# Two transformer blocks in one kernel: x is turned in two parts, eight tiles ahead of the next matrix product and eight inside its first chunk

## The reference

```python
# first block
h = rms_norm(x, g_pre_mix) * (1.0 + scale_m) + shift_m
z = h @ w_in                       # then latent attention and gated linear attention
o = concat([o_mla, o_gla]) @ w_out
x = x + gate_m * rms_norm(o, g_post_mix)
h = rms_norm(x, g_pre_ffn) * (1.0 + scale_f) + shift_f
f = (silu(h @ w_ffn_gate) * (h @ w_ffn_up)) @ w_ffn_down      # width 5632
x = x + gate_f * rms_norm(f, g_post_ffn)
# second block: 16 meta rows are put ahead of x, 272 rows in all
m = hybrid_mixer(rms_norm(h, g_pre_mix_2)) @ w_out_2
h = h + rms_norm(m, g_post_mix_2)
g = causal_dwconv(rms_norm(h, g_pre_ffn_2) @ w_gate_2, w_ffn_conv_2)   # 3 taps
f = (silu(g) * (rms_norm(h, g_pre_ffn_2) @ w_up_2)) @ w_down_2         # width 5632
h = h + rms_norm(f, g_post_ffn_2)
```

## Time and profile before

| | us |
|---|---|
| median of three runs | 2478.99 |
| the profiled execution: its own time | 2478.26 |
| its span, first to last instruction | 2476.5 |
| TensorE busy in the span | 2337.7 (94%) |
| VectorE busy | 1523.0 (61%) |
| ScalarE busy | 1073.7 (43%) |
| mean granted TensorE clock | 0.969 of full |

### The profile page before, as it was taken

How to read it: one execution, slowest core, us unless ns; L and a number is a source line. 1 busy time by engine, 2 the same in 40 slices (tenths; PEclk the granted TensorE clock), 3 DMA queues, 4 the chain that set the end, 5 groups by cost and what they waited for, 6 DMA issues and landing times.

```text
span 2476.5 us, 41603 instructions
## 1 busy us (share of the span) xinstructions
PE 2337.7 (94%) x16266; PEld 2169.9 (88%) x16266; DVE 1523.0 (61%) x1703; ACT 1073.7 (43%) x1235; POOL 123.0 (5%) x246
## 2 busy tenths in 40 slices
PE   3999989799999999999899999997999999999997
PEld 3899668799998899988699995796999988999976
DVE  7988688645554476644645994445655644566545
ACT  5463253544443344433544436345444433344433
POOL 0000013000001100001200000000000011000010
PEclk9999999999999999999999997798999999999999
DMA  9988749555555588745464550153555555555552
GB/s 397 421 325 334 314 179 369 168 186 186 186 186 193 181 290 284 272 166 193 124 204 153 187 178 25 69 186 103 181 175 186 184 180 195 187 174 181 187 186 103
DMA packets 162949, 506.35 MB, mean 204 GB/s; under 512 B 8110, under 2 KB 12494, under 8 KB 134046
## 3 DMA queue, kind: packets, MB, share of 16 engines
q1 hardware_dynamic: 161536, 500.28, 57.5%
q0 software_dynamic: 752, 3.47, 0.5%
q10 hardware_dynamic: 576, 1.44, 0.2%
HBM read 503.06 MB, written 2.10 MB: 204 GB/s over the span
## 4 chain that ended last, share of the span: by engine, by line
PE 83%; DMA 6%; DVE 6%; ACT 3%; issue 1%; SPq 0%; ACTq 0%; DVEq 0%
PE pb L547 19%; PE pb L534 18%; PE pb L536 18%; PE pb L535 18%; DMA raw<-w_in 3%; DMA raw<-w_out 2%; DMA raw<-w_ada 1%; PE pb L513 1%; PE pb L515 1%; PE pb L514 1%; DVE wlo L430 1%; PE pb L664 1%; ACT whi L423 1%; DVE x L1545 1%; DVE raw L441 1%
## 5 line engine op out<-in xcount | busy, mean ns | idle before, releaser
L430 DVE TENSOR_TENSOR wlo<-raw,whi 128x1024 fp32r<-128x1024 f32 (+1 forms) x712 | 861.7, 1221 | 770.5 <-ACT whi L423 770.1
L423 ACT ACTIVATE whi<-raw 128x1024 fp32r<-128x1024 f32 (+1 forms) x712 | 744.1, 1054 | 1077.6 <-PE pb L536 712.5
L534 PE MATMUL pb<-xh,whi 128*128 128x256 f32 (+2 forms) x3760 | 1066.6, 284 | 5.5 <-DVE xl L1736 2.5
L535 PE MATMUL pb<-xl,whi 128*128 128x256 f32 (+2 forms) x3760 | 1066.5, 284 | 0.0
L536 PE MATMUL pb<-xh,wlo 128*128 128x256 f32 (+2 forms) x3760 | 1065.8, 283 | 0.0
L534 PEld LDWEIGHTS pb<-xh,whi 128*128 128x128 f32 x3760 | 712.7, 190 | 6.8 <-DVE wlo L430 3.0
L535 PEld LDWEIGHTS pb<-xl,whi 128*128 128x128 f32 x3760 | 713.9, 190 | 0.0
L536 PEld LDWEIGHTS pb<-xh,wlo 128*128 128x128 f32 x3760 | 712.5, 190 | 0.0
L547 PE MATMUL pb<-whi,stg 128*128 128x512 f32 x1664 | 450.4, 392 | 17.2 <-DVE wlo L430 5.7
L547 PEld LDWEIGHTS pb<-whi,stg 128*128 128x128 f32 x1664 | 313.6, 189 | 86.2 <-issue 9.1
L547 PE MATMUL pb<-wlo,stg 128*128 128x512 f32 x832 | 257.9, 391 | 0.0
(11 more groups left out here) (352 smaller groups left out, 1678.1 us busy)
## 6 DMA issues: line engine op xcount, KB each, us to landing
raw<-w_ada SPq DMA_DIRECT2D x79, 1024.0 KB, 7.3
raw<-w_ffn_gate SPq DMA_DIRECT2D x44, 1024.0 KB, 5.2
raw<-w_ffn_up SPq DMA_DIRECT2D x44, 1024.0 KB, 5.2
raw<-w_ffn_down SPq DMA_DIRECT2D x44, 1024.0 KB, 4.8
raw<-w_gate SPq DMA_DIRECT2D x44, 1024.0 KB, 5.1
raw<-w_up SPq DMA_DIRECT2D x44, 1024.0 KB, 5.1
raw<-w_down SPq DMA_DIRECT2D x44, 1024.0 KB, 4.8
raw<-w_in SPq DMA_DIRECT2D x40, 1024.0 KB, 5.1
```

The source lines that it names most:

```text
L423: act.activation(to, src, ACT.Copy).then_inc(hi_ready, 1)
L430: dve.tensor_tensor(to, src, hi, ALU.subtract).then_inc(raw_done, 1)
L534: mm(o, whi[:, s, t], xh[:, k, c0:c1], start=(k == 0), stop=False)
L535: mm(o, whi[:, s, t], xl[:, k, c0:c1], start=False, stop=False)
```

## The change

TensorE turns only the tiles 0 to 7 between the stages (in changes 1 to 3; the turn at the kernel's start stays). Tiles 0 to 3 go to banks 4 to 7, tiles 4 to 7 to banks 0 to 3. The chunk starts after eight evictions. Tiles 8 to 11 are turned behind half 1 of that chunk and tiles 12 to 15 behind half 3, both into banks 4 to 7, which this chunk doesn't write. For that the first pair of each feed-forward stands outside the loops, on TensorE, ScalarE and VectorE. ScalarE and VectorE have the roundings of the weight halves 4 to 7 between the parts of x in the same order: half 4 ahead of tile 8, halves 5 to 7 ahead of tile 12.

In change 1 the post norm has another order. VectorE multiplies row 0 by its gain and adds it to x before it touches row 1; ScalarE sums the squares of row 1 first, and VectorE multiplies row 1 after that. A square root of a scalar that nobody reads stands ahead, so the activation table is loaded before the first sum of squares ends. The roundings of the halves 0 and 1 go between the two sums of squares of the new x, those of 2 and 3 behind them. In change 2 the normed row 0 comes before the meta rows.

```diff
@@ chunk (and w_in_chunk)
-            if behind is not None and h == behind[0]:
-                behind[1]()
+            if behind is not None and h in behind:
+                behind[h]()
@@ which bank, which order of rows, one turn
+    def turn_bank(n, k):
+        if n == 0:
+            return k % 8
+        return 4 + k if k < 4 else k - 4 if k < 8 else 4 + k % 4
+    def turn_rows_of(n):
+        rows = pre_rows(n)
+        return rows if n < 2 else rows[1:] + rows[:1] if n == 3 else [rows[1], rows[0], rows[2]]
+    def turn(n, k, row, last):
+        r, c, _, src = row
+        p = pt(pb[:, turn_bank(n, k), c:c + r], src[:, k * P:(k + 1) * P], kc[0:r, K_ID:K_ID + r])
+        if last:
+            p.then_inc(sem("turned"), 1)
@@ pe_turn_rows
-        order = [(k, j) for j in range(len(rows)) for k in range(8)]
-        order += [(k, j) for k in range(8, KT) for j in range(len(rows))]
...
-        pe.wait_ge(sem("turned_out"), KT * n + (12 if n else KT))
+        for j, row in enumerate(rows):
+            pe.wait_ge(sem("normed"), NORMED_AT[n] + j + 1)
+            for k in range(8):
+                turn(n, k, row, j == len(rows) - 1)
...
+        else:
+            pe.wait_ge(sem("turned_out"), KT * n + 8)
+    def pe_turn_more(n):
+        def four(k0, ready):
+            pe.wait_ge(sem("turned_out"), KT * n + ready)
+            rows = turn_rows_of(n)
+            for k in range(k0, k0 + 4):
+                for j, row in enumerate(rows):
+                    turn(n, k, row, j == len(rows) - 1)
+        return {1: lambda: four(8, 4), 3: lambda: four(12, 12)}
@@ act_turned, dve_split_x
         for k in range(KT):
+            for h in {8: (4,), 12: (5, 6, 7)}.get(k, ()):
+                between(h)
             act.wait_ge(sem("turned"), KT * n + k + 1)
...
-        for j in range(4):
-            if j < 2:
-                first((2 * j, 2 * j + 1))
+        for j, hs in enumerate(((0, 1), (2, 3), (4,), (5, 6, 7))):
+            first(hs)
             dve.wait_ge(ready, before + 4 * j + 4)
@@ pe_ffn
+            elif g == 0:
+                pair(0, behind=pe_turn_more(2 * b + 1))
+                with pe.Fori(1, n) as i:
+                    pair(i)
@@ ScalarE, change 1
-        act_row_stats(4, [(0, pb[:, 0:4, :])], lambda t: (sem("o_taken"), POST_AT[4] + 1))
-        first_hi(U_FFN, W_FFN, hs=(0, 1))
-        act_row_stats(4, [(1, pb[:, 4:8, :])], lambda t: (sem("o_taken"), POST_AT[4] + 2))
+        act.activation(stat[:, 4, 3:4], stat[:, 4, 3:4], ACT.Sqrt, bias=eps)
+        act_row_stats(4, [(t, pb[:, 4 * t:4 * t + 4, :]) for t in range(NT)],
+                      lambda t: ((used, W_FFN) if t else (sem("o_taken"), POST_AT[4] + 1)))
+        act_norm_stats(1, lambda t: (sem("post4"), t + 1), lambda: first_hi(U_FFN, W_FFN, hs=(0, 1)))
@@ VectorE, change 1
-            dve.wait_ge(*((used, W_FFN) if t else (sem("rows_done"), 1)))
+            dve.wait_ge(*((sem("rms"), RMS_AT[4] + 2) if t else (sem("rows_done"), 1)))
             dve_gained(4, pb[:, 4 * t:4 * t + 4, :], by_bank(adaA[:, :]), by_bank(xs[:, t, :]))
-        for t in range(NT):
             dve_post(4, t, xs[:, t, :], x[:, t, :], (sem("o_taken"), POST_AT[4] + t + 1), t + 1)
```

More of the change, by code:

```diff
@@ L630, in act_norm_stats @@
             rows = rows[1:] + rows[:1] * (n - 2)
-        act_row_stats(n, rows, ready)
+        act_row_stats(n, rows[:1], ready)
+        behind_first()
+        act_row_stats(n, rows[1:], ready)
     SWAPPED = {6: NT + 1}
@@ L672, in act_turned @@
+    def pe_turn_more(n):
+        def four(k0, ready):
+            pe.wait_ge(sem("turned_out"), KT * n + ready)
+            rows = turn_rows_of(n)
+            for k in range(k0, k0 + 4):
+                for j, row in enumerate(rows):
+                    turn(n, k, row, j == len(rows) - 1)
+        return {1: lambda: four(8, 4), 3: lambda: four(12, 12)}
+    def act_turned(n, width, scale=None, shift=None, between=lambda h: None):
         for k in range(KT):
+            for h in {8: (4,), 12: (5, 6, 7)}.get(k, ()):
+                between(h)
@@ L707, in body @@
             end(i)
+        if split > 4:
+            body(a0, at, lambda: halves(16, 20, a0, at), lo=split)
+            a0 += 1
         with act.Fori(a0, a1 - 1) as i:
@@ L711, in act_pairs, with dve_pairs @@
         body(a1 - 1, at_last, then, in_last)
-    def dve_pairs(u, w, a0, a1, mid, end, then, ada=None):
+    def dve_pairs(u, w, a0, a1, mid, end, then, ada=None, split=4):
         def halves(lo, hi, i, at):
@@ L731, in dve_pairs @@
         at = with_ada if ada else in_row
+        if split > 4:
+            body(a0, at, lambda: halves(16, 20, a0, at), split)
+            a0 += 1
         with dve.Fori(a0, a1 - 1) as i:
@@ L991, in pe_ffn, with pair @@
                 pe.wait_ge(sem("part_done"), 4 * (2 * b + g) - 2)
-            def pair(i, u=u, w=w, c=c, gated=gated, at=in_row, nu=8):
+            def pair(i, u=u, w=w, c=c, gated=gated, at=in_row, nu=8, behind=None):
                 pe.wait_ge(*gated(i))
-                chunk(u, w, 0, *gate_cols, at, 0, i=i, nu=nu, x_split=None if g else 8 * b)
+                chunk(u, w, 0, *gate_cols, at, 0, i=i, nu=nu, x_split=None if g else 8 * b,
+                      behind=behind)
                 pe.wait_ge(sem("h_done"), c + i)
@@ L1985, in _ @@
         pe_turn_rows(2)
-        chunk(U_WIN2X, W_WIN2X, 0, 0, T2, nf=3, width=3 * P, x_split=4)
+        chunk(U_WIN2X, W_WIN2X, 0, 0, T2, nf=3, width=3 * P, x_split=4, behind=pe_turn_more(2))
         with pe.Fori(0, 5) as i:
@@ L1997, in _ @@
             at_least(pe, sem("oT_out"), c - 1)
-            chunk(U_WOUT2 + 4 * c, W_WOUT2 + 8 * c, 4 * (c % 2), 0, NQ, behind=None if c else (FH // 2 - 1, pe_turn_yd))
+            chunk(U_WOUT2 + 4 * c, W_WOUT2 + 8 * c, 4 * (c % 2), 0, NQ, behind=None if c else {FH // 2 - 1: pe_turn_yd})
         for k in range(KT):
@@ L2124, in _ @@
         act_norm_stats(2, lambda t: (sem("post5"), t))
[L2125 to L2128 removed]
+        act_turned(2, T2, lambda k: col("g_pre_mix_2", k), between=lambda h: first_hi(U_WIN2X, W_WIN2X, n=6 * P, hs=(h,)))
         first_hi(U_WIN2, W_WIN2)
```

49 lines of the change are left out of this document (18 added, 31 removed).

## The result

| | us |
|---|---|
| before, median of 17 runs | 2478.99 (2475.08 to 2483.00) |
| changed kernel, median of 17 runs | 2484.98 (2482.26 to 2488.67) |
| ratio, 95% interval | 1.0026 (1.0019 to 1.0032) |
| predicted | 2480.2, range 2476.6 to 2484.0 |

The changed kernel is slower by some 6 us (4.7 to 7.9); forecast were 1.3 us, and the time lies 1 us above the range. Its profiled execution took 2485.14 us, with a span of 2483.3, 6.8 more than before, at a mean granted clock of 0.966.

A forecast was written before the change was run, and what follows sets the result against it. TensorE, busy for 94% of the span, was taken as the bound. Changes 1, 2 and 3 at -0.9, +2.4 and -0.2 made +1.3 us, 2479.6 profiled; with the median 0.7 above, 2480.2, range 2476.6 to 2484.0.

The forecast's parts named there:

- The chain of change 1, and the starts: Chunks of changes 1, 2, 3 start 3.6, 1.5, 2.1 us sooner; 1.7 in change 1 from new order and table.
- The late turns of change 1: Inside change 1's chunk: sixteen late turns at 0.109 us each, 1.7 us lost.
- no wait inside the chunks: Inside the first chunks of changes 1 and 2: TensorE doesn't wait for x_split, with 1 us to spare.
- The late turns of changes 2 and 3: In each chunk: sixteen turns at 0.109 us and eight of meta rows at 0.08, 2.4 us lost.
- the sum: All three changes of stage: -0.9, +2.4 and -0.2, together +1.3 us.
- a block of 1.6 us: Late turns inside chunks: such a block would show the forecast wrong; expected 0.9 in change 1, 1.2 in the others.
- the high end: Change 2's late turns: upper limit of the loss, 4.1 us, what the last eight tiles took before.
- The clock: Chunks of changes 1, 2, 3 at half clock 2.3, 3.4, 2.5 us: 1.0 lost, 1.5 lost, 0.5 won.
- My bounds: Clock term's limits: change 1 0 to 2.5 us lost, change 2 0 to 2.9, change 3 1.6 won to 1.0 lost.
- The clock stays low longer: Rival, three chunks at the high clock bounds: +0.6, +3.8, +1.3, together +5.7 us, 2484.7, slower; chance 0.09.
- late turns at the old pace: Rival: TensorE pays waits beside matmuls; the three places lose 1.5, 1.7, 1.7 us more, +6.2, 2485.2; chance 0.07.

The follow-up runs named there:

- e1: Kernel before with only change 1's new post norm order, all turns as before; 2475.84 us, ratio 0.9991 to the kernel before.
- e3: Changed kernel with each block of late turns ordered row block by row block; 2483.57 us, ratio 1.0020 to the kernel before.
- e10: Changed kernel with twelve identity turns in each pause and late turns ordered row block by row block; 2475.74 us, ratio 0.9987 to the kernel before.
- e5: Changed kernel with twelve unused identity turns in TensorE's pause ahead of each of the three chunks; 2480.29 us, ratio 1.0008 to the kernel before.
- e2: Changed kernel with change 1's post norm as before, all late turns kept; 2486.22 us, ratio 1.0040 to the kernel before.
- e6: e5 plus 18, 64 and 60 identity turns ahead of the first turns of x in changes 1, 2 and 3; 2487.21 us, ratio 1.0040.
- e7: Changed kernel with tiles 8 to 11 turned in the pause, only 12 to 15 inside the chunk, row blocks apart; 2476.76 us, ratio 1.0001.
- e9: Kernel before with e1's post norm; in change 1 only, tiles 8 to 11 turned in the pause, 12 to 15 in the chunk; 2477.57 us, ratio 0.9989.
- e11: e9 with 64 and 60 identity turns ahead of the turns of changes 2 and 3; 2475.20 us, ratio 0.9984 to the kernel before.
- e8: e1 with 18, 64 and 60 identity turns ahead of the first turns of x in changes 1, 2 and 3; 2476.69 us, ratio 0.9992.

## Why the prediction was wrong

- *The chain of change 1, and the starts.* Right. The chunks start 3.5, 1.4 and 2.0 us sooner; forecast were 3.6, 1.5 and 2.1. e1 shows the 1.6 us of the post norm by itself.
- *The late turns of change 1.* Right: two blocks of 0.79 us (forecast 0.87). So was "no wait inside the chunks".
- *The late turns of changes 2 and 3.* **Here the sum failed.** "Sixteen at 0.109 and eight at 0.08" makes 2.4 us a place. The four blocks took 2.02 to 2.04 us each, 8.1 in all where the sum had 4.8: 3.3 us too little. The prediction's own sign of being wrong, a block of 1.6 us, came. I had taken the price of two kinds of turn, each from a stretch of its own kind, for their price when mixed. The trace of before had the mixed ones: I read 4.1 us for the last eight tiles of change 2 and made it the high end, put down to waits. It was the pace itself: a tile every 0.53 us before and in the changed kernel, beside evictions and without them. Shown by e3 and again by e10 (1.29 to 1.31 a block).
- The Trainium skill ("TensorE: Matmul & The Clock Gate", Part 2, "Step-by-step: what each phase is for") says that a load goes ahead of running matmuls where row groups don't conflict or the background buffer takes it, and that the row count doesn't matter for its time. The trace agrees on the second half: a load took 0.14 us with 128 rows and with 16 (rows under e3). It is the first that decides here: where the row count changes, the load doesn't go ahead, and a block costs 0.75 us more. Which of the two conditions fails there no run here shows.
- *The clock.* Right in kind: all three chunks start low, and a microsecond of it costs 0.44 (e5: 13.7 us less of it, 6.1 us less in the sums). **Wrong in size, and this is the second step that failed**: 4.4, 4.1 and 5.9 us low where I had taken 2.3, 3.4 and 2.5. That is a loss of 4.6 us where the sum had 2.0. My bounds (5.7, 6.6 and 6.0 us low by their prices) held all three; inside them I took values with little to go by. That the pause is the cause is shown for changes 2 and 3: with it empty the chunks were low for 4.1 to 4.9 and 5.9 us (changed kernel, e2, e3), with twelve empty turns in it for 0 to 0.8 and 0 (e5, e10, and e6, which has more of them ahead). In change 1 it is not the whole cause: with the pause empty the chunk was low for 3.4 to 5.8 us in four traces, with it filled for 0 in three (e5, e7, e10) and for 3.4, 3.4 and 4.3 in three others (e6, e9, e11).
- *What I had not counted*: 0.1 us for each return from a block to the chunk, 0.6 in all (the first matmul behind a block stands 0.2 from the next, not 0.12).
- Put together: 1.3 + 0.3 (starts) + 3.3 (pace) - 0.1 (change 1's blocks) + 2.6 (clock) + 0.6 (joints) = 8.0, the places' sum. Less the 1.2 elsewhere these are 6.8, the difference of the spans.
- *The rivals.* "The clock stays low longer" (2484.7) and "late turns at the old pace" (2485.2) both came within 0.3 us of the measured 2485.0, and that is luck: each named one half of the cause in more than its true size. The first had 5.7 us for the sum with the blocks as forecast; the second named the pace with a wrong reason (waits) and in all three places, where it held in two. Their chances were 0.09 and 0.07, taken one at a time; that both could come in part was in no case.
- *Two slips* bore on nothing. The bounds of the first rival make 18.3 us at half clock, not 17; and the clock came back in change 1 of the kernel before after 16 turns, not 14.

## What to carry to other kernels

Work that is moved into a dense stream costs what it costs there in its own order: measure the pace of the exact sequence (here mixed row counts) in the trace, and don't add up paces of pure ones. A stream that starts sooner behind a pause of TensorE pays for its start with the clock: try to fill the pause, with turns that have to be made anyway (e7) or with empty ones (e5). Here twelve empty turns kept the chunks of changes 2 and 3 at full clock or nearly, one block was not enough in change 3, and in change 1 either worked in half of the traces. Read the gain at the place in the trace, since medians that scatter like these can't show two microseconds.

## What the runs showed of the hardware

- Where a turn of 128 rows stands next to one of 16 or 2, the starts are 0.15 to 0.20 us apart, against 0.11 among turns of 128 rows and 0.06 to 0.08 among the small ones (e3); at the change the weight load doesn't go ahead of the running matmul.
- 64 and 60 identity turns in the wait for x cost no time where they stand, and the sums are shorter by 1.1 and 3.1 us in changes 2 and 3 (e8 against e1). Turns alone bring the clock up: in e8 it rose at 1209.4, and TensorE had done nothing but turns since 1206.5.
- The same instructions got different clocks: change 1 of e7 and e9. It differed behind a pause elsewhere too: in the changed kernel, after TensorE was nearly idle for 3.5 us in the middle of the first feed-forward, it ran low:

```profile
1092.30:1095.80 3.50, 0.63 (x2) 0.00 (x0) 1.96 (x2) 2.73 (x2) 0.00 (x0) 1.00 0.78 257
1096.00:1099.20 3.20, 3.20 (x8) 2.55 (x9) 0.00 (x0) 0.00 (x0) 0.00 (x0) 0.52 0.05 18
```

and in the trace of before the same stretch ran at full clock:

```profile
1098.00:1101.20 3.20, 3.20 (x16) 2.61 (x15) 0.00 (x0) 0.00 (x0) 0.00 (x0) 1.00 0.00 0
```

The stretch from change 1 to change 2 is 721.4 us in five traces (before, e1, e5, e8, e10) and 723.0 in the eight others. All eight have these 3.4 us at half clock and the five have none, and 3.4 us cost 1.5 at 0.44: this is the difference. With one trace of each kernel, whether it goes by kernel or by run stays open. The stretches ahead of change 1 and between changes 2 and 3, which no edit touches, range from 437.0 to 442.9 and from 436.7 to 442.2. Here the clock isn't all: ahead of change 1 e3 and e7 both have 23.9 us at half clock and take 438.5 and 440.6. So the totals scatter by some 10 us, while a place whose code and clock are the same agrees within 0.5. Among the 12 runs of e10 the mean clock and the span go together (0.967 with 2481.7, 0.973 with 2471.1); among the runs of the kernel before they do so only loosely. What decides it in a run wasn't tried.
